# Expert lists built ahead of the loop, expert outputs added on the core into three row accumulators

## What is computed

```python
def moe(x, w_router, router_bias, w_gate_e, w_up_e, w_down_e, w_gate_s, w_up_s, w_down_s):
    t = x.reshape(-1, D_MODEL)
    scores = jax.nn.sigmoid((t @ w_router).astype(jnp.float32))
    ...                      # 8 groups of 8 experts, the best 4 groups, in them the best 8 experts
    w_sel = w_sel / jnp.sum(w_sel, -1, keepdims=True) * ROUTED_SCALE
    gates = jnp.sum(jax.nn.one_hot(top_e, N_EXPERTS, dtype=jnp.float32) * w_sel[..., None], axis=1)
    def expert_step(acc, xs):
        wg, wu, wd, g = xs
        h = jax.nn.silu(t @ wg) * (t @ wu)
        return acc + (h @ wd) * g[:, None].astype(t.dtype), None
    routed, _ = lax.scan(expert_step, jnp.zeros_like(t), (w_gate_e, w_up_e, w_down_e, gates.T))
    shared = (jax.nn.silu(t @ w_gate_s) * (t @ w_up_s)) @ w_down_s
    return (routed + shared).reshape(shp)

x = layer_norm(ALPHA * x + moe(x, ...), ln2_g, ln2_b)
```

## Time and profile before

| | us |
|---|---|
| median of 3 runs | 1369.98 (1368.73 to 1371.9) |
| the profiled execution | 1368.96 |
| its span, first to last instruction | 1367.1 |
| mean granted clock of PE | 0.957 of full speed |

### The profile page before, as it was taken

One profiled execution on the slowest core, in us unless ns is written; L12 is line 12 of the kernel. 1 busy time (PEld: TensorE's weight loads), 2 busy tenths in 40 slices (PEclk: granted clock), 3 DMA queues, 4 the chain that ended last, 5 costly groups with the idle time before them and its releaser, 6 DMA issues.

```text
span 1367.1 us, 18465 instructions
## 1 busy us (share of the span) xinstructions
PE 1237.0 (90%) x6931; PEld 972.6 (71%) x6931; DVE 775.5 (57%) x1095; ACT 543.4 (40%) x722; POOL 406.6 (30%) x385
## 2 busy tenths in 40 slices
PE   6999788899999989879999999999999999999980
PEld 6999566899999986346666666666666666666750
DVE  3124794631234345258776766666666666667735
ACT  4213573522214121134544444444444444445522
POOL 2000342210110114334433333433444433333223
PEclk9999997799999988989999999999999999999995
DMA  9941301022325038158999999999999999999944
GB/s 287 216 108 33 102 1 70 17 92 63 95 90 193 6 133 337 50 201 302 369 356 342 344 339 344 340 339 342 346 350 344 342 335 340 338 344 348 356 97 155
DMA packets 91616, 314.74 MB, mean 230 GB/s; under 512 B 15698, under 2 KB 48644, under 8 KB 66324
## 3 DMA queue, kind: packets, MB, share of 16 engines
q1 hardware_dynamic: 72160, 260.25, 50.2%
q0 software_dynamic: 18688, 53.37, 19.0%
q10 hardware_dynamic: 708, 0.28, 0.1%
HBM read 284.30 MB, written 45.22 MB: 241 GB/s over the span
## 4 chain that ended last, share of the span: by engine, by line
PE 79%; DVE 10%; issue 5%; DMA 2%; ACT 2%; POOL 2%; DVEq 0%; ACTq 0%; POOLq 0%
PE bank L1928 27%; PE bank L1948 16%; PE bank L1665 10%; PE bank L1664 10%; PE bank L1823 4%; DVE onehot L1504 4%; PE bank L1891 3%; PE bank L1679 3%; PE bank L1853 2%; DVE L L1259 1%; PE bank L1844 1%; DVE mx L1265 1%; DMA y_rows<-ysb,idx_u 1%; PE bank L1870 1%; DVE ysb L1544 1%
## 5 line engine op out<-in xcount | busy, mean ns | idle before, releaser
L1528 DVE TENSOR_TENSOR wgu_lo<-wgu,wgu_hi 128x4096 fp32r<-128x4096 f32 x64 | 282.6, 4416 | 2.7 <-ACT wgu_hi L1128 2.7
L807 POOL TENSOR_TENSOR spare<-spare 128x1 f32<-128x1 f32 x128 | 119.8, 936 | 445.0 <-DMA y_rows<-ysb,idx_u 408.9
L1948 PE MATMUL bank<-wd,hT 128*128 128x512 f32 x512 | 230.1, 592 | 0.9 <-DVE hT L1538 0.9
L1128 ACT ACTIVATE wgu_hi<-wgu 128x4096 fp32r<-128x4096 f32 x63 | 227.4, 3609 | 0.0
L1928 PE MATMUL bank<-wgu_hi,xgT 128*128 128x512 f32 x512 | 205.2, 401 | 2.6
L1928 PE MATMUL bank<-wgu_hi,xgT_lo 128*128 128x512 f32 x512 | 200.0, 391 | 0.0
L1928 PE MATMUL bank<-wgu_lo,xgT 128*128 128x512 f32 x512 | 199.9, 390 | 0.0
L1132 ACT ACTIVATE silu<-bank 128x256 f32<-128x256 f32 x64 | 24.5, 383 | 367.3 <-PE bank L1928 367.3
L1948 PEld LDWEIGHTS bank<-wd,hT 128*128 128x128 f32 x512 | 96.7, 189 | 98.0 <-issue 92.0
L1544 DVE COPY ysb<-bank 128x512 f32<-128x512 f32 x64 | 44.3, 692 | 163.2 <-PE bank L1948 163.2
L1928 PEld LDWEIGHTS bank<-wgu_hi,xgT 128*128 128x128 f32 x512 | 96.3, 188 | 23.4 <-issue 0.5
(11 more groups left out here) (287 smaller groups left out, 2431.6 us busy)
## 6 DMA issues: line engine op xcount, KB each, us to landing
wgu<-in_w_gate_e_dram SPq DMA_DIRECT2D x64, 1024.0 KB, 9.2
wgu<-in_w_up_e_dram SPq DMA_DIRECT2D x64, 1024.0 KB, 13.8
wd<-in_w_down_e_dram SPq DMA_DIRECT2D x64, 1024.0 KB, 7.8
raw<-in_w_in_dram SPq DMA_DIRECT2D x16, 1024.0 KB, 5.9
raw<-in_w_proj_a_dram SPq DMA_DIRECT2D x4, 1024.0 KB, 5.1
raw<-in_w_out_dram SPq DMA_DIRECT2D x4, 1024.0 KB, 5.2
x_lo_kept<-xT_lo SPq DMA_DIRECT2D x1, 2304.0 KB, 10.7
x_lo_back<-x_lo_kept SPq DMA_DIRECT2D x1, 2304.0 KB, 8.4
```

Source lines behind the costliest of these rows:

```text
L807: pool.tensor_tensor(spare[:, i:i + 1], spare[:, 0:1], spare[:, 0:1], ALU.mult).then_inc(s, 1)
L1128: act.activation(wgu_hi[u % 2][:], wgu[u % WSLOTS][:], ACT.Copy).then_inc(hi_by_act, 1)
L1528: v.tensor_tensor(wgu_lo[u % WSLOTS][:], w_[:], wgu_hi[u % 2][:].bitcast(F32), ALU.subtract).then_inc(lo_by_dve, 1)
L1948: last = mm(bank[3 + h][:, :], hT[:, u % 2, j, :], wd[slot][:, j, h * 512:(h + 1) * 512], start=j == 0, stop=j == FE // P - 1)
```

## The change

- **Lists.** `R`, the one-hots, `token_list` and the index operations go. Each token's eight experts and its positions in their lists give eight slot numbers (`slot_u`); POOL writes the token's number to these slots of a DRAM table `owner` by 5 x 8 indirect scatters of 4 bytes a row, ahead of the loop. The table was filled with an index past the tokens before. One DMA reads back `idx_all`, the index columns of all 64 experts.
- **Gates.** They are stored as 64 more columns of the rows of x in DRAM (`DG = D + E`), come with the x gather, and `hidden` takes its column there.
- **Adding y.** There are three accumulators `y_rows[0..2]` in DRAM. Expert e uses accumulator e % 3 (the last four e % 2). POOL gathers its rows to `yg`, DVE adds both halves from PSUM (two operations of 512 columns), and POOL scatters them back plainly, without trash rows. A gather waits for the last scatter to its accumulator. Accumulators 1 and 2 are zeroed by POOL, ten DMAs, where one stood.
- **Order.** POOL per step: y gather of e, x gather of e+3, scatter of e-1; the `spare` operations go. hT is copied by ACT. DVE's step: `xt_evac`, `weights_lo`, `hidden`, `y_add`. All loops are unrolled.
- **Shared expert.** Its product and sum move from POOL (and two ACT copies) to DVE; `places` is moved ahead by one tile.
- **End.** SP loads three accumulators (the third early), DVE adds them per tile.

The diff, cut to its core:

```diff
+            def sh_sum(t):
+                ...
+                for j in range(2):
+                    v.scalar_tensor_tensor(sy[0:w, t % 2, j * 512:(j + 1) * 512], x1[0:w, t, j * 512:(j + 1) * 512], ALPHA,
+                                           bank[j][0:w, :], ALU.mult, ALU.add).then_inc(sy_dve, 1)
...
+            then(v.scalar_tensor_tensor(slot[:], bank[7][:, 0:NT * E].rearrange("p (t e) -> p t e", t=NT), -float(E),
+                                        slot_base[:]..., ALU.mult, ALU.add))
+            then(v.tensor_tensor(slot[:], slot[:], smask[:], ALU.mult))
+            for t in range(NT):
+                v.max(top8[:, t, :], slot[:, t, :]).then_inc(dve, 1)
+            v.tensor_scalar(slot_u[:], top8[:], -1.0, float(FAR_SLOT), ALU.mult, ALU.add).then_inc(route_dve, 1)
...
+            for i in range(1, NACC):
+                for t, (a, w) in enumerate(TILES):
+                    pool.dma_start(y_rows[i][a:a + w, :], sgln[0:w]...).then_inc(y_zeroed, 16)
...
+            pool.wait_ge(route_dve, 1)
+            for t, (a, w) in enumerate(TILES):
+                for r in range(8):
+                    pool.indirect_dma_start(out=owner, out_offset=bass.IndirectOffsetOnAxis(slot_u[0:w, t, r:r + 1], 0),
+                                            in_=token_id[0:w, t:t + 1], in_offset=None).then_inc(owner_written, 16)
+            pool.wait_ge(owner_written, 16 * NT * 8)
+            pool.dma_start(idx_all[:, :], owner.rearrange("(t p e) a -> t p (e a)", t=NT, p=P)[0]).then_inc(idx_landed, 16)
...
+            for e in range(XGSLOTS - 1):
+                gather_x(e, xg_in[e], idx_all[:, e:e + 1])
+            for e in range(E):
+                if e >= NACC:
+                    pool.wait_ge(y_put[acc[e]], 16 * (turn[e] - 1))
+                gather_y(acc[e], idx_all[:, e:e + 1])
+                n = e + XGSLOTS - 1
+                if n < E:
+                    if e >= 1:
+                        pool.wait_ge(h_by_dve, e)
+                        pool.wait_ge(ex_xt, e)
+                    gather_x(n % XGSLOTS, xg_in[n % XGSLOTS], idx_all[:, n:n + 1])
+                if e >= 1:
+                    pool.wait_ge(y_by_dve, 2 * e)
+                    scatter_y(acc[e - 1], idx_all[:, e - 1:e])
...
+            def y_add(e, i):
                 v.wait_ge(ex_dn, e + 1)
-                if free:
-                    v.wait_ge(y_added, (e - 1) * 16)
-                v.tensor_copy(ysb[:, u % 2, 512:1024], bank[4][:, :]).then_inc(y_by_dve, 1)
+                for h in range(2):
+                    c = slice(h * 512, (h + 1) * 512)
+                    v.tensor_tensor(yg[i][:, c], yg[i][:, c], bank[3 + h][:, :], ALU.add).then_inc(y_by_dve, 1)
...
+            for e in range(E):
+                if e + 1 < E:
+                    xt_evac(e + 1, e + 1)
+                    weights_lo(e + 1, e + 1)
+                hidden(e, e, slice(D + e, D + e + 1))
+                if e >= 1:
+                    v.wait_ge(y_got[acc[e - 1]], 16 * turn[e - 1])
+                    y_add(e - 1, acc[e - 1])
...
+                then(v.tensor_tensor(x1[0:w, t, :], x1[0:w, t, :], y_other[0][0:w, t, :], ALU.add))
+                then(v.tensor_tensor(x1[0:w, t, :], x1[0:w, t, :], y_other[1][0:w, t, :], ALU.add))
                 stats(t, 1)
```

More of the change, by code:

```diff
@@ L22 @@
 BUCKET_FAR = 128
-UNROLL = 8
 WSLOTS = 4
@@ L267, in hybrid_layer @@
     y_at = h0 + wslot_bytes
-    ysb = place("ysb", [P, 2, D], F32, y_at)
+    yg_at = [y_at, y_at + D * 4, j0 + JBYTES - D * 4]
+    yg = [place(f"yg{i}", [P, D], F32, yg_at[i]) for i in range(NACC)]
+    assert j_at[0] <= yg_at[2]
+    acc = [e % NACC if e < E - 4 else e % 2 for e in range(E)]
+    turn = [acc[:e + 1].count(acc[e]) for e in range(E)]
+    uses = [acc.count(i) for i in range(NACC)]
     assert y_at + 2 * D * 4 <= h0 + RAW * DC * SB * 4
@@ L292, in hybrid_layer @@
     rsum = place("rsum", [P, NT], F32, f0 + 6784)
-    gates = place("gates", [P, NT, E], F32, f0 + 6848)
-    rest = place("rest", [P, NT, E], F32, f0 + 8192)
+    slot = place("slot", [P, NT, E], F32, f0 + 8192)
     smask = place("smask", [P, NT, E], F32, f0 + 9536)
@@ L1159, in _ @@
-            for e in range(UNROLL):
-                step(e, e, 0, first=e == 0, free=e >= 3)
-            with act.Fori(1, E // UNROLL - 1) as i:
-                for u in range(UNROLL):
-                    step(i * UNROLL + u, u, i)
-            for e in range(E - UNROLL, E):
-                step(e, e % UNROLL, E // UNROLL - 1, last=e == E - 1, ahead=e + 2 < E)
-            ex_y(E - 1, E - 1)
-            act.wait_ge(y_added, 16 * E)
+            for e in range(E):
+                if e + 1 < E:
+                    ex_xt_evac(e + 1, e + 1)
+                if e >= 1:
+                    ex_ht_evac(e - 1, e - 1)
+                    act.wait_ge(h_by_dve, e)
+                ex_silu(e)
+                if e + 2 < E:
+                    weights_hi(e + 2, (e + 2) // WSLOTS + 1)
@@ L1169, in _ @@
+            ex_ht_evac(E - 1, E - 1)
+            for i in range(NACC):
+                act.wait_ge(y_put[i], 16 * uses[i])
             most_r = act.value_load(most[0:1, 0:1], min_val=0, max_val=TOK)
@@ L1578, in _ @@
-            for e in range(UNROLL):
-                step(e, e, first=e == 0, wait=e + IDX_AHEAD >= UNROLL, free=e >= 3)
-            with v.Fori(1, E // UNROLL - 1) as i:
-                for u in range(UNROLL):
-                    step(i * UNROLL + u, u)
-            for e in range(E - UNROLL, E):
-                step(e, e % UNROLL, ahead=e + IDX_AHEAD < E, last=e == E - 1)
-            ht_evac(E - 1, E - 1)
-            y_evac(E - 1, E - 1)
-            v.wait_ge(y_added, 16 * E)
+            sh_sum(4)
@@ new lines, in _ @@
+            v.wait_ge(x1_written, 16 * NT)
+            xt_evac(0, 0)
+            for e in range(E):
+                if e + 1 < E:
+                    xt_evac(e + 1, e + 1)
[4 more added lines that the diff above has]
+                    y_add(e - 1, acc[e - 1])
+            v.wait_ge(y_got[acc[E - 1]], 16 * turn[E - 1])
+            y_add(E - 1, acc[E - 1])
@@ L1589, in _ @@
+            for i in range(NACC):
+                v.wait_ge(y_put[i], 16 * uses[i])
             most_r = v.value_load(most[0:1, 0:1], min_val=0, max_val=TOK)
@@ L1883, in places @@
                 last.then_inc(pos_done, 1)
-            def token_list(e, u, wait=True):
-                pe.wait_ge(hot_by_dve, e + 1)
-                if wait:
-                    pe.wait_ge(sum_by_dve, e)
-                for t in range(NT):
-                    last = mm(bank[7][:, 0:6], onehot[:, u % 4, t, :], R[:, t, bass.ds(e, 1), :],
-                              start=t == 0, stop=t == NT - 1)
-                last.then_inc(ex_list, 1)
             pe.wait_ge(shared_landed, 48)
@@ L1923, in gate_up @@
                 pe.wait_ge(lo_by_dve, e + 1)
-                if wait:
+                if not (isinstance(e, int) and e == 0):
                     pe.wait_ge(h_by_dve, e)
```

471 lines of the change are left out of this document (187 added, 284 removed).

## The result

The changed kernel takes **1407.07 us** (median of 4, 1405.87 to 1410.22) against 1369.72 for the kernel before on the same chip: a ratio of 1.027 with a 95% interval of 1.025 to 1.030. It is 37 us slower; forecast were 8. Its profiled execution has a span of 1404.4 us.

What follows compares the result with a forecast made beforehand. PE at 11.59 us a step was taken as the bound before, loads on the lower DMA engines after. Head +6, the loop at 11.45 a set and tail +10.5 gave net +8.2, 1378 us; range 1345 to 1410.

Steps and rivals of the forecast that it cites:

- 11.45 us a set: Loop after: an expert's weight loads, slowed by the lower half of the DMA engines, take 11.45 us; bounds 10.95 and 12.0.
- the tail's +10.5: After the last gate/up: shorter scatter -3.8, accumulator loads +1.5, DVE additions +12.8, together +10.5 us; bounds +7 and +15.
- the head's +6: Before the loop: POOL's 40 indirect scatters and DVE's copies make the first gate/up 6 us later; bounds -4 and +24.
- No wait here ends last at steps of 10 to 12 us: Loop after: waits for scatters and gathers on POOL and DVE don't set the pace; the loads end last.
- PE at 11.59: Loop before: PE's step of 11.59 us, 1.55 of it for list, one-hot and register addresses, bounds the loop.
- 11.50 us a set: Loop before: the engines needed 667.2 us for 58 weight sets, 11.50 each, 0.1 us behind PE.
- Which DMA engines: Row gathers: rows go to engines by partition, so one half of the engines carries nearly the whole gather, 8 rows each.
- The half share: Two row gathers running alone show an engines' share of 0.51, read as half of the engines working.
- The packet sum: Loop after, a low engine's transfers per step: weights 7.68, x gather 1.36, y gather 1.28, plain scatter 1.28, in all 11.60 us.
- A: Loop: rows spread evenly over 16 engines or queues overlap better, PE stays the bound at 10.04 a step, 1303; chance 0.20.
- B: Loop: loads bound, but the lower half gains, a set at 10.95 us, 29 less, 1349; chance 0.07.
- C: Head: 4-byte scatters at 1.58 us and more behind DVE's copies, +20 us, 1398; chance 0.07.

## Why the prediction was wrong, by its steps

The direction was right, the size was not: 37 us slower and not 8. Three terms were mis-sized. The loop's 11.45 us a set took 11.62, the tail's +10.5 was +20.0, the head's +6 was +10.9. And the step "No wait here ends last at steps of 10 to 12 us" failed: PE waited 71 us in the loop for x rows.

**What bounded the kernel before: half right.** PE at 11.59 stands (the plain scatter left the steps at 11.58). "11.50 us a set" for the loads was wrong: it was PE's pace read off the loads, because a load is issued when PE frees its slot. With the same rows and the accumulation left out the loads kept up with 10.80. A landing rate is the rate of whoever asks, as long as nothing waits for the transfer. What stood right behind PE was the serial accumulating scatter, for whose landings POOL waited 306 of the 532 us from 704 to 1236; I had that wait in view and didn't ask what it would do in a faster loop.

**Which DMA engines: right.** The half share was rows dealt by partition; spreading them gave 55 us. That it is the partitions is shown by that run; the single engines are not seen.

**The loop after: the right resource, the wrong wait, and 0.17 us a set too little.** The transfers on the lower engines bind, as forecast: only their relief moved the steps by more than 0.1 us. But what PE waited for in the kernel after was the x gather's landing, and ACT's wait for up loads, forecast as the last one, was 42 us in 46 steps. The packet sum gave 11.60. The up loads of experts 5 and 63 landed at 645.03 and 1319.26 us, 11.62 a set; I moved from 11.60 to 11.45 only because of the false 11.50. Over 58 sets that is 10.1 of the 14.7 us by which this stretch missed. 0.5 more lie ahead of them (the up load of 5 landed 25.2 us behind the first gate/up, and not 24.7), and 4.1 behind the last load: from its landing to the end of gate/up 63 (1337.95) 18.7 us and not 14.6, for gate/up 62 had itself waited for its rows. The near hit of 11.60 is in part luck: the same prices give 12.48 for the kernel before, which ran at 11.58 without waiting for a load. For the kernel without y gathers they give 10.32, and its steps are 10.40. PE's own pace of 10.04 held for four steps and not ten; with x first it held for eight, with rows spread for seventeen.

**"No wait here ends last": wrong, but cheap.** I gave the x gather three steps in hand. It stands behind the y gather, which stands behind the landing of a scatter 16.7 us old, so it had 15 us for a landing of 14.4. And I priced the y gather's issue by a row in which DVE was idle: 1.08 against 4.05. The order was visible in the stream. Mended alone, the first is worth 7 us and the second nothing, because the transfers hold the pace either way; with the rows spread both together are worth 12.6.

**The head: +10.9 instead of +6.** The scatters ran as forecast but for their size. POOL's group ahead of the loop, 500 to 700 us:

```profile
L823 POOL DMA_INDIRECT owner<-token_id,slot_u x40 | 43.9, 1097 | 58.3 <-DVE slot_u L1486 46.4 <-issue 11.9
```

They fill 543.5 to 599.3, 55.8 us where 48 were reckoned: 1.27 each (0.97 and 0.30 between) and not 1.2; the eight of 64 rows 1.21 and not 0.8, so such an issue hardly depends on its rows; two stretched by DVE's copy and lo split by 5.5 and not 3. The first rows came at 607.86 and not at 603 (600 and 3 for DVE's copies), which is the 4.9 us that the head missed by. The zeroing and SP's small transfers cost nothing that shows.

**The tail: +20.0 instead of +10.5.** By the marks: last gate/up to last landing 13.5 (18.4 before), -4.9 where -3.8 stood; landing to the first tile 8.8 instead of 3.6, +5.2 where +1.5 stood, of which 1.5 is SP, whose read of the list length had moved behind the waits, with its branch, and 3.7 the doubled loads; the rest 44.1 instead of 24.4, +19.7 where +12.8 stood, of which 6.0 is the second addition beside POOL's in three tiles. I had named that stretch as a bound of the term and not counted it. Taking POOL's part away gave 4.9 of it back.

**The rivals.** A (PE stays the bound, 1303) needed the rows even over 16 engines. They were not; made so by hand, with the order on POOL and the split besides, the loop came close to PE's pace, at 1339.6 with this head and tail. The Trainium skill, "DMA: Bandwidth & Descriptors", section "Anatomy of one DMA", prices by total bytes: with the lists on half of the engines the loop stays far from that rule, and with the rows spread it comes near. B and C didn't happen; C's dear head was half true.

## What to carry to other kernels

Read a transfer's need for time from a stretch where something waits for it, or from its packets on the fullest engine; the rate at which it lands elsewhere is the pace of the compute. Short lists that start at partition 0 load half of the DMA engines; deal them over all partitions early. A kernel at two or three bounds at once answers a single relief with nothing, or with a loss when the next bound is a serial chain: try reliefs in pairs, and follow every moved read and wait in the tail, where each microsecond counts in full.

## What the hardware showed that was not expected

- An indirect DMA's issue on POOL takes 1.0 us, but 4.4 when it starts 0.9 us into DVE's 4.42 us subtraction of two SBUF operands, and it ends 0.9 us behind it. With the same work in four operations it takes 1.21 us.
- A scatter that accumulates in DRAM lands alone after 5.9 to 6.4 us with 72 rows and 6.0 to 6.6 with 128; among the loads after 9.8 to 11.4. A plain one lands alone after 3.2 to 3.4.
- Writing out a hardware loop made PE's step 10.80 instead of 11.58 us, and the kernel 30 us slower.
- A 32-bit product of 512 columns takes PE 0.86 us at full clock, against 1.24 for DVE's addition of 1024 columns: PE is no cheap adder of such tiles.
